# Two transformer blocks in one launch: the opening's queue order, the phases of the first projection and the modulation sums are rearranged

## What is computed

```
c_act = silu(c)
for i in range(2):
    mod = c_act @ ada_w[i] + ada_b[i]                 # 2048 -> 3 * 2048
    shift, scale, gate = split(mod, 3)
    h = rmsnorm(x, norm_g[i]) * (1 + scale) + shift   # 256 x 2048
    y = retention_branch(h, ...) if i == 0 else mla_branch(h, ...)
    x = x + gate * y
return rmsnorm(x, final_norm_g)
```

## Time and profile before

| | |
|---|---|
| median of 3 runs | 2247.28 us (2246.63 to 2249.52) |
| profiled execution, own time | 2248.64 us |
| its span in the trace | 2246.9 us |
| PE busy | 2211.2 us (98%) |
| DVE busy | 1488.8 us (66%) |
| ACT busy | 1039.2 us (46%) |
| DMA moved | 501.92 MB, mean 223 GB/s |

### The profile page before, as it was taken

The page is one execution under the profiler, slowest core; times in us unless marked ns, Lnnn a source line. Parts: engine busy times, 40 slices in busy tenths (PEclk is TensorE's granted clock), DMA queues, the critical chain, the costliest instruction groups (busy, mean ns, idle before and its releaser), DMA issues.

```text
span 2246.9 us, 26966 instructions
## 1 busy us (share of the span) xinstructions
PE 2211.2 (98%) x10384; PEld 1836.0 (82%) x10384; DVE 1488.8 (66%) x1901; ACT 1039.2 (46%) x1353; POOL 97.4 (4%) x79
## 2 busy tenths in 40 slices
PE   5999999999999999999999999999999999999999
PEld 4878887878887788989888888888888888888887
DVE  7898778777876978655685655655555455555554
ACT  4544354443444545545455455444444444344442
POOL 0000000000000000000021100000100000000000
PEclk8999999999999999999999999999999999999999
DMA  9998577878887769735456554566666656666664
GB/s 348 372 328 306 173 259 273 305 247 310 296 291 247 277 218 340 249 116 174 150 176 222 169 179 137 178 189 187 186 188 187 195 187 184 195 186 192 190 187 141
DMA packets 139795, 501.92 MB, mean 223 GB/s; under 512 B 15633, under 2 KB 16145, under 8 KB 139153
## 3 DMA queue, kind: packets, MB, share of 16 engines
q1 hardware_dynamic: 139376, 499.99, 67.0%
q10 hardware_dynamic: 290, 0.21, 0.0%
HBM read 498.04 MB, written 2.10 MB: 223 GB/s over the span
## 4 chain that ended last, share of the span: by engine, by line
PE 90%; DVE 4%; DMA 3%; ACT 1%; issue 1%; SPq 0%; POOL 0%; DVEq 0%; ACTq 0%
PE ps L1016 74%; PE ps L1027 7%; PE ps L1094 3%; PE ps L1041 2%; DMA raw<-in_ret_in 2%; DVE wlo L1585 1%; DMA arena<-in_ret_in 1%; DVE raw L1592 1%; DVE arena L1792 0%; PE ps L1191 0%; DVE x L1800 0%; DVE alo L1585 0%; DMA raw<-in_ada_t 0%; PE ps L1169 0%; PE ps L1168 0%
## 5 line engine op out<-in xcount | busy, mean ns | idle before, releaser
L1585 DVE TENSOR_TENSOR wlo<-raw,whi 128x1024 fp32r<-128x1024 f32 (+1 forms) x711 | 867.8, 1225 | 577.6 <-ACT whi L1273 574.6
L1273 ACT ACTIVATE whi<-raw 128x1024 fp32r<-128x1024 f32 (+1 forms) x711 | 740.1, 1045 | 806.8 <-PE ps L1016 640.6
L1016 PE MATMUL ps<-whi,ahi 128*128 128x512 f32 x2482 | 787.6, 397 | 4.6 <-ACT arena L1378 1.8
L1016 PE MATMUL ps<-wlo,ahi 128*128 128x512 f32 x2482 | 770.4, 390 | 2.0 <-DVE wlo L1585 1.9
L1016 PE MATMUL ps<-whi,alo 128*128 128x512 f32 x2482 | 770.6, 390 | 0.0
L1016 PEld LDWEIGHTS ps<-wlo,ahi 128*128 128x128 f32 x2482 | 466.1, 188 | 102.5 <-DVE wlo L1585 3.6
L1016 PEld LDWEIGHTS ps<-whi,alo 128*128 128x128 f32 x2482 | 466.6, 188 | 98.4
L1016 PEld LDWEIGHTS ps<-whi,ahi 128*128 128x128 f32 x2482 | 456.3, 188 | 96.0 <-issue 3.8
L1592 DVE SCALAR_TENSOR_TENSOR raw<-raw,arena 128x1024 f32<-128x1024 f32 x184 | 223.6, 1217 | 0.1
L1027 PE MATMUL ps<-whi,ahi 128*128 128x512 f32 x254 | 99.6, 392 | 0.0
L1027 PE MATMUL ps<-wlo,ahi 128*128 128x512 f32 x254 | 98.9, 389 | 0.0
(11 more groups left out here) (212 smaller groups left out, 1344.4 us busy)
## 6 DMA issues: line engine op xcount, KB each, us to landing
raw<-in_mlp SPq DMA_DIRECT2D x256, 512.0 KB, 3.9
raw<-in_ret_in SPq DMA_DIRECT2D x188, 512.0 KB, 5.0
raw<-in_ada_t SPq DMA_DIRECT2D x184, 512.0 KB, 5.1
raw<-in_in SPq DMA_DIRECT2D x80, 512.0 KB, 4.3
raw<-in_ret_out SPq DMA_DIRECT2D x64, 512.0 KB, 4.9
raw<-in_mla_in SPq DMA_DIRECT2D x48, 512.0 KB, 4.7
raw<-in_mla_out SPq DMA_DIRECT2D x32, 512.0 KB, 4.2
raw<-in_out SPq DMA_DIRECT2D x32, 512.0 KB, 3.6
```

What stands on the lines that cost most here:

```text
L1016: mm = e.matmul(acc_[:, :], (ahi, alo, ahi)[m][:, slot, kb, tb * P:(tb + 1) * P], parts[m][:, chunk(n)], start=first and m == 0, stop=False)
L1273: e.activation(high(i)[:, 0:ncol], raw_of(n)[:, 0:ncol], ACT.Copy).then_inc(*s_hi.up(i))
L1585: e.tensor_tensor(low(i)[:, 0:ncol], raw_of(n)[:, 0:ncol], high(i)[:, 0:ncol].bitcast(F32), ALU.subtract).then_inc(*s_lo.up(i))
```

## The change

- `PHASES` becomes two phases, of 6 and 10 blocks; in the second the order of groups is "v next", "qk", "v", "qk next", "g". 9 groups are emptied in place of 13.
- A modulation tile is 2048 wide (1 MB, two lanes side by side), one DVE instruction and one DMA in place of two. Bytes stay the same.
- `mods` moves to ACT: two activations on 128 x 1 with scale and bias in place of three DVE instructions; POOL multiplies bias and gain once ahead.
- Loads are still written as far ahead as the ring allows, but consumption only up to 3 weights beyond TensorE's while fewer than some 50 are used (`LAZY`).
- In the opening the first modulation tile is loaded ahead of x; TensorE runs 5 extra matmuls; ACT takes all of silu(c) before its squares; DVE sums tile 0 between its two squares and tile 1 before `dg`; turns 0 and 1 stand ahead of the split of w0 on ACT, turns 2 and 3 ahead of the first block, turns 4 to 7 among the side jobs after the first phase's pair of groups.
- The tiles of blocks 6 to 15 are due between w12 and w44 (before: blocks 4 to 15 between w8 and w60).

```diff
-PHASES = [range(0, 4), range(4, 10), range(10, 16)]
+PHASES = [range(0, 6), range(6, 16)]
+BESIDE, LAZY = 12, 50
-ORDERS = [("qk", "v", "g", "qk next", "v next"), ("v next", "qk next", "g", "v", "qk"),
-          ("qk", "v", "qk next", "v next", "g")]
+ORDERS = [("qk", "v", "g", "qk next", "v next"), ("v next", "qk", "v", "qk next", "g")]
...
+    for j in range(20):
+        due.setdefault(BESIDE + j * 17 // 20 * 2, []).append((PHASES[1][j // 2], j % 2))
     for i in range(first):
+        if i < BESIDE and i % 2 == 0:
+            plan += [("adt", 0, i // 2, c) for c in range(2)]
+        plan += [("adt", 0, kb, c) for kb, c in due.get(i, ())]
         plan.append(w[i])
...
+    def pump(upto, made=None):
+        while at["next"] < len(plan) and at["weight"] <= upto:
+            n = at["next"]
+            at["next"] += 1
             do("load", n)
+            at["weight"] += plan[n][0] == "w"
+        if made is None:
+            made = upto if at["used"] > LAZY else min(upto, at["used"] + 2)
+        consume(made)
+    def consume(upto):
+        while at["made"] < at["next"] and at["split"] <= upto:
+            make()
+    def make():
+        n = at["made"]
+        at["made"] += 1
+        if plan[n][0] == "w":
+            do("split", at["split"], n)
+            at["split"] += 1
+            if 2 < at["split"] <= BESIDE and at["split"] % 2 == 0:
+                mod_to(at["split"] // 2 - 1)
+            return
+        _, layer, kb, c = plan[n]
+        do("adt", layer, kb, c, n)
+        if c == 1 and layer == 0 and kb in PHASES[0]:
+            do("mods", layer, kb, 1)
+            ready.append(range(kb, kb + 1))
...
+    at["next"] = 1
+    do("load", 0)
     do("opening", got)
...
-    pump(0, 3)
+    pump(7, -1)
+    make()
+    do("rows_mean")
+    make()
     do("norm_diag", "h0")
-    pump(0, 6)
     turn_first(0)
+    turn_first(1)
+    consume(0)
     mod_to(0)
-    turn_first(1)
+    consume(1)
+    turn_first(2)
+    turn_first(3)
...
         side_by_side(order[:2], kbs, held)
         if ph == 0:
+            side += [lambda k2=k2: turn_first(k2) for k2 in range(4, 8)]
...
+            # ACT
+            def mods(layer, k0, n):
+                bias, gain = ada_bias(layer), COLS["norm_g"][0] + layer * 16
+                w.wait_ge(*s_pool.on("one more"))
+                w.wait_ge(*s_ada.on(("adt", layer, k0 + n - 1, 1)))
+                for kb in range(k0, k0 + n):
+                    e.activation(mod[:, layer, 0, kb:kb + 1], sums[:, layer, kb, 0:1], ACT.Identity, bias=bias[:, 0, kb:kb + 1])
+                    m = e.activation(mod[:, layer, 1, kb:kb + 1], sums[:, layer, kb, 1:2], ACT.Identity, scale=cols[:, gain + kb:gain + kb + 1], bias=bias[:, 1, kb:kb + 1])
...
+            # DVE
+            def adt(layer, kb, c, n):
+                r = raw_of(n)
+                late = layer == 1 and c == 2
+                w.wait_ge(*s_raw[lanes[n]].on(n))
+                w.wait_ge(*s_act.on("c_late" if late else ("c_wide", 3)))
+                e.scalar_tensor_tensor(out=r, in0=r, scalar=1.0, in1=c_late if late else c_wide, op0=ALU.mult, op1=ALU.mult,
+                                       accum_out=sums[:, layer, kb, c:c + 1]).then_inc(*s_ada.up(("adt", layer, kb, c)))
```

More of the change, by code:

```diff
@@ L177, in schedule @@
     side, urgent, ready, modulated = deque(), deque(), deque(), set()
-    at = {"next": 0, "weight": 0, "used": 0, "ahead": 0}
+    at = {"next": 0, "weight": 0, "made": 0, "split": 0, "used": 0, "ahead": 0}
     met = {}
@@ L194, in pump @@
             do("load", n)
[L195 to L210, removed]
+            at["weight"] += plan[n][0] == "w"
[19 more added lines that the diff above has]
+            ready.append(range(kb, kb + 1))
+        elif c == 1 and kb % 2:
+            do("mods", layer, kb - 1, 2)
+            if layer == 0:
+                ready.append(range(kb - 1, kb + 1))
+        elif c == 2 and kb % 4 == 3:
+            do("gate_sum", layer, kb // 4)
+            urgent.append((at["used"] + 3, lambda layer=layer, j=kb // 4: gate_row(layer, j)))
     def gate_row(layer, j):
@@ L796, in lane_of @@
             return n % EARLY if n < 24 else (n - 24 + 24 % EARLY) % RAW
-        lanes = [lane_of(n) for n in range(len(plan))]
-        lane_before = [max((m for m in range(max(0, n - EARLY), n) if lanes[m] == lanes[n]), default=None) for n in range(len(plan))]
-        def raw_of(n):
-            lane = lanes[n]
-            if lane < RAW:
-                return raw[:, lane, :]
-            a = (dtab, sg, v, v_next)[(lane - RAW) // 2]
-            return flat(a)[:, (lane - RAW) % 2 * 1024:(lane - RAW) % 2 * 1024 + 1024]
+        lanes, lanes_before, held_by = [], [], {}
+        at_lane = 0
+        for n, item in enumerate(plan):
+            size = 1 if item[0] == "w" else 2
+            at_lane += at_lane % size
+            own = [lane_of(at_lane + i) for i in range(size)]
+            lanes.append(own[0])
+            lanes_before.append(sorted({held_by[lane] for lane in own if lane in held_by}))
+            held_by.update((lane, n) for lane in own)
+            at_lane += size
+        def raw_of(n):
+            lane, width = lanes[n], 1024 if plan[n][0] == "w" else 2048
+            a = flat(raw) if lane < RAW else flat((dtab, sg, v, v_next)[(lane - RAW) // 2])
+            first = (lane if lane < RAW else (lane - RAW) % 2) * 1024
+            return a[:, first:first + width]
         R0 = Region()
@@ L1065, in opening @@
                 w.wait_ge(*s_pool.on("ones"))
+                for _ in range(5):
+                    e.matmul(empty(got[0])[:, 0:P], ones[:, :], ones[:, :], start=True, stop=True)
                 w.wait_ge(*s_in["c_row"].on("in"))
@@ L1409, in v_copy @@
             def v_copy():
[L1410 removed]
+                w.wait_ge(*s_act.on(("part", LAST["v next"], "v next", 1, 1)))
                 w.wait_ge(*s_att.on(("ret_values", 0, 1, 1)))
@@ L1595, in mods @@
-            def mods(layer, k0, n):
-                ks, last = slice(k0, k0 + n), k0 + n - 1
-                o, oa = mod[:, layer, :, ks], mod[:, layer, 1, ks]
-                halves = sums[:, layer, ks, 0:4].rearrange("p k (c h) -> p c k h", c=2)
-                w.wait_ge(*s_ada.on(("adt", layer, last, 1, 1)))
-                e.tensor_tensor(o, halves[:, :, :, 0], halves[:, :, :, 1], ALU.add).then_inc(*s_vec.up(("mod red", layer, last)))
-                w.wait_ge(*s_vec.on(("mod red", layer, last)))
-                w.wait_ge(*s_pool.on("one more"))
-                e.tensor_tensor(o, o, ada_bias(layer)[:, 0:2, ks], ALU.add).then_inc(*s_vec.up(("mod sum", layer, last)))
-                w.wait_ge(*s_vec.on(("mod sum", layer, last)))
-                e.tensor_tensor(oa, oa, col("norm_g", layer * 16 + k0, n), ALU.mult).then_inc(*s_vec.up(*[("mod", layer, kb) for kb in range(k0, k0 + n)]))
+                w.wait_ge(*s_act.on("c_late" if late else ("c_wide", 3)))
@@ new lines, in gate_sum, with row_square @@
+                e.tensor_tensor(gate_col[:, layer, ks], sums[:, layer, ks, 2], ada_bias(layer)[:, 2, ks], ALU.add).then_inc(*s_vec.up(("gate_sum", layer, j)))
+            def row_square(tb):
+                xs = x[:, tb, 1024:2048]
+                w.wait_ge(*s_in[f"x{tb}1"].on("in"))
+                e.scalar_tensor_tensor(out=flat(kT), in0=xs, scalar=1.0, in1=xs, op0=ALU.mult, op1=ALU.mult, accum_out=stat[:, 2 * tb + 1:2 * tb + 2]
+                                       ).then_inc(*s_vec.up(("square", "h0", tb)))
@@ L1653, in norm_diag @@
                     mean_square(src, o)
-                mean(src, o)
+                    w.wait_ge(*s_vec.on(("sums", src)))
+                    mean(src, o)
                 w.wait_ge(*s_pool.on(("rstd", src)))
```

102 lines of the change are left out of this document (40 added, 62 removed).

## The result

| | before | after | ratio (95% interval) |
|---|---|---|---|
| median of 4 runs | 2246.95 us | 2284.41 us | 1.0163 (1.0145 to 1.0181) |
| range of the runs | 2246.60 to 2249.52 | 2280.80 to 2286.92 | |
| profiled execution: own time, span | 2248.64, 2246.9 | 2286.92, 2285.2 | |

The forecast was 2253.0 us in a range of 2241 to 2261. The sign was right and the size was not: 37 us came where 6 were forecast. The profiled execution of after lies 2.5 us above its median, so spans read from the trace exaggerate the loss by about 1 us in all.

What follows compares the result with a forecast made beforehand. PE, busy 2211.2 of 2246.9 us, was taken to bound the kernel. w0's later start (+4.7 us) and +0.8 to +1.0 after it make +5.7, added to the median: 2253 us, range 2241 to 2261.

Steps and rivals of the forecast that it cites:

- w16 to w79: Weights w16 to w79: PE doesn't wait for DMA's 62 tiles; up to 6 us of loss as the upper bound.
- rival 3: Between w16 and w46 the six lanes starve PE, by the upper 6 us: 2259 us; chance 0.07.
- Later stages ... nothing: Stages after w79: same PE work, DVE relieved of 60 fixed costs of about 0.08 us, no change in time.
- `mods` now stands on ACT's queue: Blocks 1 to 5: `mods` sits between a block's sums and its splits, so DVE waits for ACT's split.
- Blocks 1 to 5: First phase: a cycle of 9.55 us per block, PE waiting 4.8 us for block 1, block 5 ready at 72.8.
- the opening: Start to w0: the split loses its cover, so w0 starts at 26.0 us, not 21.3.
- bank waits at w12 and turn 4: Before w16: PE waits 1.7 and 1.6 us for banks that ACT empties behind splits.
- POOL's power hides under tile 1: Opening: POOL's power runs beneath DVE's sum of tile 1, with `dg` done at 18.4 us.
- DMA is about seven tiles ahead: At w16: the lead of landed tiles, given in support of no PE wait from there to w79.
- Rival 2: Blocks 1 to 5: DVE does not wait, five cycles at 7.2 us, 12.8 us sooner: 2240 us; chance 0.19.
- Rival 1: Costs taken at their upper side, as for `mods` and turns, give the loss back: no change, 2247 us; chance 0.22.
- Rival 4: Blocks 1 to 5: PE's clock falls in every cycle, 10.9 us a pair, +12.6 us: 2266 us; chance 0.05.

Runs made afterwards that it cites:

- the repaired kernel: The changed kernel with modulation tiles in halves, eight lanes in place of six and `mods` back on DVE: 2248.6 us, 1.0007 of the kernel before.

## Why the prediction was wrong

**The failed step is "w16 to w79"**: "62 tiles are to land until w46, 79 us of DMA, and PE takes 81.6 us ... I put this at no wait, with up to 6 us of loss". It priced DMA at the 1.28 us a tile of the opening, where 14 lanes are open. In a ring of six lanes the rate is the lanes' bytes over the time that a lane is held: 6 x 0.524 MB at 328 GB/s is 9.6 us of holding on average. At that rate 62 tiles take 99 us, not 79. Even the kernel before, with narrow tiles in the same six lanes, moved 381 GB/s from 100 to 140 us, at which 62 tiles take 85 us, more than PE's 81.6. The mechanism stood there as rival 3, "The six lanes starve PE", with a price of 6 us and a chance of 0.07; it was mis-sized, since its price came from slack against an unhindered DMA, and since nothing was put beside the idle time of its waits. Stage 2 lost 15.6 us and missed the forecast by 17.4. The runs show that the ring was short: with eight lanes 12.4 us of the stage come back, with halves 6.5, and with both and `mods` on DVE all of it.

**"Later stages ... nothing" failed too**, by 8.6 us over stages 4 and 5, and the rest of "w16 to w79" (stage 3) by 4.8. In stage 4 the cause is shown: with `mods` on DVE it is 535.4 to 535.7 us in four kernels, with `mods` on ACT 539.2 to 543.4 in five. The step that "`mods` now stands on ACT's queue" was priced for blocks 1 to 5 and not for the second layer, where the same two instructions stand ahead of splits. In stage 5, kernels with narrow tiles are at 1444.5 to 1445.0 and those with wide ones at 1445.3 to 1447.5: up to 3 us that go with width, by comparison of single executions, with no single wait behind it; the runs of after alone spread over 6 us. In stage 3 every kernel with two phases, the repaired one too, loses 3.4 to 6.1 us. But those with three phases and the short lead lose 2.6 to 3.4 as well, and the short lead alone makes it 90.0 us for 86.6:

```profile
173.80:263.80 90.00, 87.96 (x389) 70.98 (x388) 79.03 (x107) 41.14 (x45) 0.00 (x0) 1.00 0.77 273
```

So the short lead by itself can cost some 3 us there. Where there are two phases, the stage's one large wait is this (timeline of after):

```profile
237.76 3.49 DVE L1624 TENSOR_TENSOR wlo<-raw,whi 128x1024 fp32r<-128x1024 f32 x3
...
241.16 1.28 DVE L1759 TENSOR_TENSOR arena<-ps,arena 128x512 f32<-128x512 f32 x2
242.10 1.09 PE L1125 MATMUL ps<-ident,arena 128*128 128x128 f32 x4 [3.63 <-DVE arena L1759]
```

A turn of the "qk" group waits for its last additions, which stand behind three low parts on DVE. The wait is in every kernel with two phases that was looked at here, and absent from after with the old phases, whose stage still takes 89.3 us. Nothing moved the additions alone, so how much of the stage hangs on them is not shown.

**What was right.** Blocks 1 to 5 came out by their own terms, and the opening nearly so:

| | forecast | after |
|---|---|---|
| w0 starts | 26.0 | 25.6 |
| PE waits for block 1 | 4.8 | 4.5 |
| h of blocks 1, 2, 3, 4, 5 | 36.3, 44.15, 53.7, 63.25, 72.8 | 35.8, 43.4, 52.5, 61.6, 70.8 |
| cycle | 9.55 | 9.1 |
| bank waits at w12 and turn 4 | 1.7, 1.6 | 1.0, 2.2 |
| w16 starts | 96.3 | 98.0 |

The w0 of the forecast hangs on turns 2 and 3, which were to end at 26.0. They end at 24.6, and PE then waits 1.03 us for h of block 0, which the forecast had at 25.6 and which came at 25.56: the number was near, the bound was the other one. "POOL's power hides under tile 1" failed by 0.61 us (last section). In the sum for the kernel before, w79 does not end at 264.7 but starts there (264.60): 2.6 us of other matmuls lie between w32 and w79. The same was left out on the side of after, so it cancels in the difference.

One cycle in the timeline of after, ACT, DVE and SP, 40 to 50 us:

```profile
40.27 0.29 ACT L1303 ACTIVATE mod<-sums,cols 128x1 f32<-128x1 f32 x1 [5.30 <-DVE raw L1631]
40.47 0.37 ACT L1304 ACTIVATE mod<-sums,cols 128x1 f32<-128x1 f32 x1
40.75 1.04 ACT L1312 ACTIVATE ahi<-raw 128x1024 fp32r<-128x1024 f32 x1
...
41.83 1.23 DVE L1624 TENSOR_TENSOR alo<-raw,ahi 128x1024 fp32r<-128x1024 f32 x1 [1.59 <-ACT ahi L1312]
...
47.18 0.80 SPq L990 DMA_DIRECT2D raw<-in_ada_t  x2
48.09 1.15 SPq L988 DMA_DIRECT2D raw<-in_ret_in  x2
49.28 0.08 DVE L1631 DVE_READ_ACCUMULATOR arena<-arena 128x1 f32 x1
```

ACT idles 5.30 us ahead of its two activations until the sum is done, and DVE then idles 1.59 us for the split, as forecast. The cycle is 0.4 us shorter: the pair of activations takes 0.48 us to the next start, not 0.65, and the ACT rows behind it start 0.1 us before the row ahead has ended. (The Trainium skill, ScalarE: Activation LUTs, "What ACT_TABLE_LOAD costs", gives 0.28 us for a tiny activation with a pointer for bias, 0.09 more for one more pointer and an overlap of 0.09; the rows of 0.29 and 0.37 us, 0.20 apart, agree, and by it the term would have been an estimated 0.56.) What the steps did not carry on is the last lines: the loads go out only at 47.18, when DVE gives lanes back. The window of the same stretch has DMA all but idle:

```profile
40.00:50.00 10.00, 9.20 (x40) 7.08 (x38) 7.45 (x9) 3.98 (x9) 0.00 (x0) 0.99 0.19 55
```

The forecast's "DMA is about seven tiles ahead" at w16 had not counted such stops.

**The rivals.** Rival 2 fell: DVE did wait. The short lead without `mods` on ACT had its gain, 13 us at w6, and even that was lost before w79. Rival 1 fell with the size. Rival 4 was half right: with three of the four waits for h in blocks 1 to 5 (4.52, 3.36 and 3.38 us, not the one of 1.75) PE went slowly for 3 to 4.5 us. PE's timeline behind the wait for block 3 has pairs of matmuls at 1.05 us, which are 0.62 at full clock:

```profile
52.57 0.73 PE L1045 MATMUL ps<-ahi 128*128 128x512 f32 x2 [3.36 <-DVE alo L1661]
...
54.24 1.05 PE L1045 MATMUL ps<-ahi 128*128 128x512 f32 x2
...
57.94 0.62 PE L1045 MATMUL ps<-alo,ahi 128*128 128x512 f32 x2
```

In blocks 1 to 5 this hid behind the cycle, as the prediction argued. In stage 2 nothing hid it, but there it is some 3 of the 15.6 us. (The rule of the Trainium skill that the prediction weighed, TensorE: Matmul & The Clock Gate, "HAM oscillation — how this bites in real kernels", bursts that each begin at half clock, agrees in part. Block 1's first pair took 1.22 us, at half clock from the start, and so did block 5's matmuls. Block 3's clock fell about 1 us after its burst began, and block 4's burst kept full clock.)

**What stays open.** Stage 2's loss can't be split exactly between width, lanes and activations, since their shares depend on each other. The 3.6 us wait in stage 3 was not tried alone, nor was the short lead undone in the changed kernel. That stage 4 takes 535.4 us in the repaired kernel and 537.4 in the kernel before has no shown cause. Before with wide tiles has 535.4 as well; what it shares with the repaired kernel, and what the four kernels at 537.4 lack, is the later tiles' place after every second weight, which was not tried alone.

## What to carry to other kernels

Ask of every plan of loads what rate it needs, and compare that with the rate that the ring of landing buffers gives in the trace, not with the rate of an opening in which all buffers are free; a wider tile that takes two places at once lowers it. An instruction of 0.3 us that waits for another engine is priced by what stands behind it in its queue, in every stage that issues it, and by the buffers that those keep. TensorE's idle time is not the whole price of its waits: stages 2, 3 and 4 here took 0.3 to 1.3 us more of busy time for each us more of idle time, and only part of that was the clock. And an early gain lasts only if the next bound has room for it: of 13 us won at w6 with six lanes and the old turns 0.8 were left at w79, and of 17 us with late turns and eight lanes 9.9.

## What the runs showed of the hardware

**POOL beside a wide DVE sum.** The power of 128 x 2 took 2.69 us after, and 0.73 us before with DVE idle (timeline of after, 15 to 18.5 us):

```profile
15.17 2.28 DVE L1631 SCALAR_TENSOR_TENSOR raw<-raw,arena 128x2048 f32<-128x2048 f32 x1
15.34 2.69 POOL L2035 TENSOR_TENSOR stat<-stat,mhalf 128x2 f32<-128x2 f32 x1 [6.76 <-DVE stat L1677]
...
18.07 0.48 DVE L1674 TENSOR_SCALAR dg<-ident,stat 128x128 f32<-128x128 f32 x2 [0.61 <-POOL stat L2035]
```

It ends 0.58 us after the sum does, as if it had begun only then; DVE idles 0.61 us for it. The Trainium skill (SBUF — State Buffer, "SBUF: two separate sides") says that a DVE instruction with two SBUF inputs and a GpSimd operation that reads SBUF exclude each other for a whole instruction, which these rows agree with; no run here moved the one away from the other.

**Size of a transfer.** The Trainium skill (DMA: Bandwidth & Descriptors, "Bandwidth") advises batches of 1 MiB and more. Here 1 MB transfers were no help at either depth of the ring: from 100 to 140 us 337 GB/s where halves gave 355 with six lanes, and with eight lanes and `mods` on DVE 375 where halves gave 392. From 140 to 180 us that last pair is the other way round, 379 and 361, in a kernel whose PE no longer idles there. These are rates of the ring and of what the plan asks for; no run shows the rate of one size of transfer by itself.
